# Two blocks of a transformer on one core: the closing norm by halves of the tokens, with GpSimd in the centring, and one ScalarE copy for both groups' turned probabilities

## The reference, cut to what matters

```python
p_s = masked_softmax(s_s, (kpos <= t[:, None])[:, :, None])
o_s = jnp.einsum('bghqn,bgqnd->bghqd', p_s.astype(v_sel.dtype), v_sel)
...
p_w = masked_softmax(s_w, wmask)
o_w = jnp.einsum('bghqk,bgkd->bghqd', p_w.astype(v_w.dtype), v_w)
```

```python
def layer_norm(x, g, b):
    xf = x.astype(jnp.float32)
    mu = jnp.mean(xf, axis=-1, keepdims=True)
    var = jnp.mean(jnp.square(xf - mu), axis=-1, keepdims=True)
    return ((xf - mu) * lax.rsqrt(var + LN_EPS) * g + b).astype(x.dtype)

x = layer_norm(ALPHA * x + sqrelu_mlp(x, mlp_w1[i], mlp_w2[i]), ln2_g[i], ln2_b[i])
```

## Time and profile before

| | us |
|---|---|
| median of 3 runs (1921.96 to 1923.71) | 1922.18 |
| the profiled execution, its own time | 1923.41 |
| its span, first to last instruction | 1921.6 |
| PE busy | 1884.6 (98%) |
| PEld busy | 1516.7 (79%) |
| POOL busy | 1077.0 (56%) |
| DVE busy | 794.2 (41%) |
| ACT busy | 431.5 (22%) |
| mean granted TensorE clock | 0.996 |

### The profile page before, as it was taken

One profiled execution on the slowest core, in us unless ns is written; L12 is line 12 of the kernel. 1 busy time (PEld: TensorE's weight loads), 2 busy tenths in 40 slices (PEclk: granted clock), 3 DMA queues, 4 the chain that ended last, 5 costly groups with the idle time before them and its releaser, 6 DMA issues.

```text
span 1921.6 us, 24551 instructions
## 1 busy us (share of the span) xinstructions
PE 1884.6 (98%) x9032; PEld 1516.7 (79%) x9032; DVE 794.2 (41%) x1305; ACT 431.5 (22%) x850; POOL 1077.0 (56%) x622
## 2 busy tenths in 40 slices
PE   7999999999999999999999999999999999999997
PEld 5878887888888888866778888887776878888885
DVE  6774432352433435688451212126523561212126
ACT  5223422310000121155140101014424140101022
POOL 5756752676657666420556556664752646666552
PEclk9999999999999999999999999999999999999998
DMA  6322321233324225210223322332321223332321
GB/s 231 112 75 92 109 89 33 88 111 100 107 77 132 93 94 199 66 45 1 77 78 98 98 87 87 97 100 76 100 88 45 77 77 99 102 98 95 98 88 44
DMA packets 46880, 176.01 MB, mean 92 GB/s; under 512 B 5200, under 2 KB 5328, under 8 KB 46032
## 3 DMA queue, kind: packets, MB, share of 16 engines
q1 hardware_dynamic: 46512, 169.55, 27.5%
q10 hardware_dynamic: 288, 5.31, 0.7%
HBM read 172.74 MB, written 2.10 MB: 91 GB/s over the span
## 4 chain that ended last, share of the span: by engine, by line
PE 95%; DVE 3%; ACT 1%; issue 1%; DMA 0%; SPq 0%; DVEq 0%
PE acc L499 17%; PE acc L500 17%; PE acc L501 17%; PE acc L526 6%; PE acc L523 6%; PE acc L522 6%; PE acc L578 1%; PE acc L579 1%; PE acc L580 1%; PE acc L1122 1%; PE acc L1124 1%; PE acc L1123 1%; PE acc L598 1%; PE acc L599 1%; PE acc L597 1%; PE misc L831 1%
## 5 line engine op out<-in xcount | busy, mean ns | idle before, releaser
L2491 POOL TENSOR_SCALAR w_hi<-raw 128x1024 fp32r<-128x1024 f32 x309 | 334.8, 1083 | 786.9 <-PE acc L526 292.9
L2493 POOL TENSOR_TENSOR w_lo<-raw,w_hi 128x1024 fp32r<-128x1024 f32 x309 | 746.9, 2417 | 25.8
L499 PE MATMUL acc<-x_hi,w_hi 128*128 128x512 f32 x872 | 343.1, 393 | 0.0
L501 PE MATMUL acc<-x_hi,w_lo 128*128 128x512 f32 x872 | 339.5, 389 | 0.0
L500 PE MATMUL acc<-x_lo,w_hi 128*128 128x512 f32 x872 | 339.4, 389 | 0.0
L1877 DVE TENSOR_TENSOR h<-acc,h 128x512 f32<-128x512 f32 x120 | 82.9, 691 | 365.3 <-PE acc L501 234.4
L499 PE MATMUL acc<-y_hi,w_hi 128*128 128x512 f32 x580 | 227.3, 392 | 0.0
L501 PE MATMUL acc<-y_hi,w_lo 128*128 128x512 f32 x580 | 225.7, 389 | 0.0
L500 PE MATMUL acc<-y_lo,w_hi 128*128 128x512 f32 x580 | 225.7, 389 | 0.0
L499 PEld LDWEIGHTS acc<-x_hi,w_hi 128*128 128x128 f32 x872 | 163.8, 188 | 35.7 <-issue 2.3
L501 PEld LDWEIGHTS acc<-x_hi,w_lo 128*128 128x128 f32 x872 | 163.6, 188 | 34.1
(11 more groups left out here) (430 smaller groups left out, 2738.0 us busy)
## 6 DMA issues: line engine op xcount, KB each, us to landing
raw<-weights_dram SPq DMA_DIRECT2D x309, 512.0 KB, 3.5
w_cmp<-w_cmp_dram ACTq DMA_DIRECT2D x1, 4096.0 KB, 16.0
h<-x_dram SPq DMA_DIRECT2D x2, 1024.0 KB, 6.1
out_dram<-h SPq DMA_DIRECT2D x8, 256.0 KB, 2.0
small<-small_dram SPq DMA_DIRECT2D x1, 1408.0 KB, 15.9
small<-small_dram ACTq DMA_DIRECT2D x1, 1088.0 KB, 5.1
mem_in<-mem_dram SPq DMA_DIRECT2D x1, 1024.0 KB, 12.9
const<-const_dram SPq DMA_DIRECT2D x1, 640.0 KB, 9.1
```

The source lines that it names most:

```text
L499: mm(out, m["w_hi"][:, slot, k], hi[:, k], start=k == 0, stop=False)
L501: last = mm(out, m["w_lo"][:, slot, k], hi[:, k], start=False, stop=k == kc - 1)
L2491: nc.gpsimd.tensor_scalar(hi, m["raw"][:, slot], 1.0, 0.0, ALU.mult, ALU.add).then_inc(sem("weights_high"), 1)
L2493: nc.gpsimd.tensor_tensor(m["w_lo"][:, slot].rearrange("p k n -> p (k n)"), m["raw"][:, slot], bf(hi), ALU.subtract).then_inc(sem("weights ...
```

## The change

**In the batch loop** VectorE's copy is gone. ScalarE copies both groups in one instruction, which waits until both are turned, and one semaphore `n_pt` takes the place of two.

**At the end** `last_tiles`, `last_sums` and two functions called `last_ln` take the place of the second half of the last MLP group and of `residual_ln`, for the last norm alone:

- t12 to t15 are made twice, first for tokens 0 to 255 and then for tokens 256 to 511, with products of 256 columns: 192 in place of 96. A tile of the second half waits until the same tile of the first half has been added to `h` (`last_taken`).
- The sums over the features are made by halves: those of the first half stand behind t12 of the second half.
- ScalarE copies the first mean to `mean` in SBUF. VectorE centres chunks 0 to 3 with it, and GpSimd, behind its last split, chunks 4 to 7 (L2691, 128x512). VectorE adds chunk 4 + j only when GpSimd has centred it (`pool_centred`).
- In the second centring VectorE has chunks 0 to 4 and GpSimd 5 to 7 (`POOL_CENTRES`, L2695, 128x256), for each half.
- `part`, the running squares and the scaled chunks are in SBUF now (`last`, laid over `x_hi` and `x_lo`, which are no longer read then). So these VectorE instructions have two tensors in SBUF as operands: L1977, L1979, L1982, L1983, L1852 (before L1760), L2000, L2003, L2012, L2026 and L2037.
- The result goes out as 16 transfers of 128 KB.

```diff
@@ n_turn, n_values (PE)
-            if b:
-                pe.wait_ge(sem("n_pt%d" % g), b)
+            if b and g == 0:
+                pe.wait_ge(sem("n_pt"), b)
...
-        for g in range(2):
-            pe.wait_ge(sem("n_pt%d" % g), b + 1)
+        pe.wait_ge(sem("n_pt"), b + 1)
@@ batch loop (ACT)
-        act.wait_ge(sem("n_turned"), 2 * b + 1)
+        act.wait_ge(sem("n_turned"), 2 * b + 2)
         if b >= 2:
             act.wait_ge(sem("n_values"), b - 1)
-        f(m["pt_n"][:, b % 2, 0, 0:n], misc[:, 0, 0:n], ACT.Copy).then_inc(sem("n_pt0"), 1)
+        f(m["pt_n"][:, b % 2, :, 0:n], misc[:, 0:2, 0:n], ACT.Copy).then_inc(sem("n_pt"), 1)
@@ batch loop (DVE)
-        dve.wait_ge(sem("n_turned"), 2 * b + 2)
-        if b >= 2:
-            dve.wait_ge(sem("n_values"), b - 1)
-        v.tensor_copy(m["pt_n"][:, b % 2, 1, 0:n], misc[:, 1, 0:n]).then_inc(sem("n_pt1"), 1)
@@ the last tiles (PE)
+    def last_sums(half):
...
+        pe.wait_ge(sem("ln_sum"), 2 * i + 2 + half)
...
+        mm(mean, ones, m["sum_h"][:, cols], start=True, stop=False)
+        pe.wait_ge(sem("last_taken"), HALF * (half + 1))
+        mm(mean, ones, m["h"][:, KC - 1, cols], start=False, stop=True).then_inc(sem("ln_mean"), 1)
+        pe.wait_ge(sem("last_added"), HALF * (half + 1))
+        mm(squares, ones, m["sum_sq"][:, cols], start=True, stop=True).then_inc(sem("last_summed"), 1)
+    def last_tiles(t0, norm):
+        for half in range(2):
+            cols = blk(half, TOK)
+            for j in range(HALF):
+                slot = (t0 + j) % RING
+                if half == 0:
+                    claim(t0 + j)
+                else:
+                    pe.wait_ge(sem("last_taken"), j + 1)
+                for k in range(KC):
+                    mm(acc[:, slot, cols], m["w_hi"][:, slot, k], y_hi[:, k, cols], start=k == 0, stop=False)
+                    mm(acc[:, slot, cols], m["w_hi"][:, slot, k], y_lo[:, k, cols], start=False, stop=False)
+                    last = mm(acc[:, slot, cols], m["w_lo"][:, slot, k], y_hi[:, k, cols], start=False, stop=k == KC - 1)
+                last.then_inc(sem("last_done"), 1)
+                if half == 0 and j == 0:
+                    sum_features(norm, 0)
+                if half == 1 and j == 0:
+                    last_sums(0)
+        last_sums(1)
@@ last_ln (ACT), its first mean and its final steps
+        f(m["mean"], misc[:, 0, :], ACT.Copy, scale=-1.0 / (HALF * P)).then_inc(sem("last_mean"), 1)
...
+        def final(half, k):
+            cols = blk(half, TOK)
+            act.wait_ge(sem("last_scaled"), KC * half + k + 1)
+            f(m["h"][:, k, cols], scaled[:, k, cols], ACT.Identity, bias=pr.col("ln2_b", KC + k))\
+                .then_inc(sem("out_ready"), 1)
@@ last_ln (DVE), the steps ahead of the first take
+        dve.wait_ge(sem("last_mean"), 1)
+        for k in range(HALF):
+            v.tensor_tensor(h[:, k], h[:, k], mean, ALU.add).then_inc(sem("ln_centred"), 1)
+        own.mark(v.scalar_tensor_tensor(part, mean, float(HALF), total, ALU.mult, ALU.add))
+        own.settle()
+        for k in range(1, HALF):
+            add_squares(name, k)
+        def taken(half, j):
+            c, cols, n = HALF + j, blk(half, TOK), HALF * half + j
+            if half == 0:
+                dve.wait_ge(sem("pool_centred"), j + 1)
+            dve.wait_ge(sem("last_done"), n + 1)
+            v.tensor_tensor(h[:, c, cols], acc[:, (t0 + c) % RING, cols], h[:, c, cols], ALU.add)\
+                .then_inc(sem("last_taken"), 1)
...
@@ behind the last split (POOL)
+    pool.wait_ge(sem("last_mean"), 1)
+    for k in range(HALF, KC):
+        nc.gpsimd.tensor_tensor(m["h"][:, k], m["h"][:, k], m["mean"], ALU.add).then_inc(sem("pool_centred"), 1)
+    for half in range(2):
+        pool.wait_ge(sem("last_mean"), half + 2)
+        for k in POOL_CENTRES:
+            nc.gpsimd.tensor_tensor(m["h"][:, k, blk(half, TOK)], m["h"][:, k, blk(half, TOK)],
+                                    m["mean"][:, blk(half, TOK)], ALU.add).then_inc(sem("pool_centred"), 1)
```

More of the change, by code:

```diff
@@ L357, in memory_map @@
     place("row_M", [S], F32, arena - 4 * S)
+    place("last", [KC + 2, S], F32, x)
     place("mn_hi", [KC, MEM], F32R, y)
@@ L410, in norm_banks @@
             return self.misc[:, 0, MEM:2 * MEM], self.misc[:, 0, 0:n], [self.misc[:, b, 0:n] for b in (3, 1, 2)]
+        if name == LAYER_NORMS[-1]:
+            return self.m["last"][:, 0], self.misc[:, 2], None
         fourth = (START[BEFORE_STAGE[name]] + 3) % RING
@@ L1080, in normed_stage @@
         sum_features(norm, 1)
+    def last_sums(half):
+        i, cols = len(LAYER_NORMS) - 1, blk(half, TOK)
+        pe.wait_ge(sem("ln_sum"), 2 * i + 2 + half)
+        mean, squares = misc[:, (1, 3)[half], cols], misc[:, (2, 0)[half], cols]
+        mm(mean, ones, m["sum_h"][:, cols], start=True, stop=False)
[22 more added lines that the diff above has]
+        last_sums(1)
     def mlp_group(name, g, norm, high, next_norm=None):
@@ L1333, in keep, with last_ln, squares, deviation @@
                 .then_inc(sem("norm_kept"), 1)
-        def final(k):
-            f(m["h"][:, k], banks[k % 3], ACT.Identity, bias=pr.col(bias, at + k)).then_inc(sem("out_ready"), 1)
-        if name in KEPT:
-            high_chunks(name, high, keep)
-        else:
-            high_chunks(name, final, None)
+        high_chunks(name, high, keep)
+    def last_ln(name):
+        logs()
+        i, rstd, scaled = LAYER_NORMS.index(name), m["last"][:, 0], m["last"][:, 2:]
+        act.wait_ge(sem("ln_mean"), 2 * i + 1)
+        f(m["mean"], misc[:, 0, :], ACT.Copy, scale=-1.0 / (HALF * P)).then_inc(sem("last_mean"), 1)
+        for k in range(HALF):
+            act.wait_ge(sem("ln_centred"), HALF * i + k + 1)
+            square(name, k, m["h"])
+        def squares(half, j):
+            cols = blk(half, TOK)
+            act.wait_ge(sem("last_taken"), HALF * half + j + 1)
+            if j < 2:
+                act.wait_ge(sem("norm_added"), chunks_before(name) + HALF)
+            else:
+                act.wait_ge(sem("last_added"), HALF * half + j - 1)
+            f(m["sq"][:, j % 2, cols], m["h"][:, HALF + j, cols], ACT.Square).then_inc(sem("last_sq"), 1)
+        def deviation(half):
+            cols = blk(half, TOK)
+            act.wait_ge(sem("ln_mean"), 2 * i + 2 + half)
+            act.wait_ge(sem("last_added"), HALF * half + 3)
+            mean = misc[:, (1, 3)[half], cols]
+            f(m["sq"][:, 0, cols], mean, ACT.Square, scale=1.0 / D).then_inc(sem("ln_mean_sq"), 1)
+            act.wait_ge(sem("pool_centred"), HALF)
+            f(m["mean"][:, cols], mean, ACT.Copy, scale=-1.0 / D).then_inc(sem("last_mean"), 1)
+            act.wait_ge(sem("ln_var"), i + 1 + half)
+            own.link(f(rstd[:, cols], rstd[:, cols], ACT.Ln, bias=LN_EPS, scale=1.0))
+            f(rstd[:, cols], rstd[:, cols], ACT.Exp, scale=-0.5).then_inc(sem("last_rstd"), 1)
+        def final(half, k):
+            cols = blk(half, TOK)
+            act.wait_ge(sem("last_scaled"), KC * half + k + 1)
+            f(m["h"][:, k, cols], scaled[:, k, cols], ACT.Identity, bias=pr.col("ln2_b", KC + k))\
+                .then_inc(sem("out_ready"), 1)
+        for j in range(HALF):
+            squares(0, j)
+        squares(1, 0)
+        deviation(0)
+        squares(1, 1)
+        for k in range(3):
+            final(0, k)
+        squares(1, 2)
+        for k in range(3, 6):
+            final(0, k)
+        squares(1, 3)
+        for k in range(6, KC):
+            final(0, k)
+        deviation(1)
+        for k in range(KC):
+            final(1, k)
@@ L2374, in mlp @@
         up(GROUPS - 1)
-        residual_ln(norm, START[name] + 16 * (GROUPS - 1) + 8, lambda c, first=None: down(GROUPS - 1, c, first))
+        close = last_ln if norm == LAYER_NORMS[-1] else residual_ln
+        close(norm, START[name] + 16 * (GROUPS - 1) + 8, lambda c, first=None: down(GROUPS - 1, c, first))
     mlp("mlp_a", "ln2a")
@@ L2530, in sync_program @@
             .then_inc(sem("weights_in%d" % slot), 16)
-    for k in range(KC):
-        sp.wait_ge(sem("out_ready"), k + 1)
-        sp.dma_start(dram["out"][:, k], m["h"][:, k]).then_inc(sem("stored"), 16)
-    sp.wait_ge(sem("stored"), 16 * KC)
+    for half in range(2):
+        cols = blk(half, TOK)
+        for k in range(KC):
+            sp.wait_ge(sem("out_ready"), KC * half + k + 1)
+            sp.dma_start(dram["out"][:, k, cols], m["h"][:, k, cols]).then_inc(sem("stored"), 16)
+    sp.wait_ge(sem("stored"), 16 * 2 * KC)
 def build(nc, dram):
```

103 lines of the change are left out of this document (93 added, 10 removed).

## The result

| | before | after |
|---|---|---|
| median, us | 1922.18 (1921.96 to 1923.71) | 1926.01 (1925.2 to 1928.49) |
| the profiled execution, its own time | 1923.41 | 1926.01 |
| its span | 1921.6 | 1924.0 |
| from VectorE's first take of the last eight tiles to the end of the span | 1921.6 - 1875.75 = 45.85 | 1924.0 - 1870.76 = 53.24 |

The ratio is 1.0021 with an interval of 1.0015 to 1.0027 (19 runs of each kernel): 3.8 us slower. The whole interval lies above 1, so the loss is real, but it has the 0.2% that the prediction calls no change (1.0020) inside it. The forecast was 2.2 us slower, 1924.4. The last line of the table is the measure to use for the end. It leaves out what happens earlier in the program, and that scatters: where the code ahead of the last tiles was the same, the first take came anywhere between 1870.4 and 1872.2 us.

A forecast was written before the change was run, and what follows sets the result against it. PE was taken as the bound, its chain covering 95% of the span. From 1922.2: -3.6 in the batch loop, +4.5 at the end, +1.3 for the clock, +2.2 in sum, gives 1924.4 us; whole range 1915.5 to 1927.5.

The forecast's parts named there:

- The batch loop: Batch loop: without VectorE's copy 3.6 us are gained (1.4 + 1.1 + 0.4 + 0.7); bounds 0 and 5.4.
- the bound that I name: Three-block batches of the loop: VectorE needs 2.65 us, so PE at 2.71 is the bound, in place of 3.12.
- The rival in which this copy eats the gain: Batch loop: each turn waits for ScalarE's wide copy, gain under 2 us; with none 1928.0, slower. Chance 0.15.
- What stands between the halves: Last tiles: VectorE and GpSimd take turns, the first take ends at 1899.9, and PE stands still for 5.2 us.
- The walk: Last tiles: following the engines' order with turns, GpSimd has 9.9 us of work and VectorE's eight instructions end at 1899.5.
- rows 9: Profile rows before: beside GpSimd, six VectorE instructions with two SBUF operands take 7.65 us where 6 x 0.6 would do.
- The rule that I weighed: GpSimd's centrings at the end: the rule would give 1.4 us each and about 0.7 us more gap; forecast used 1.2.
- The second half and behind it: End: half tiles done at 1913.0 against 1904.05; 9.0 us lost before PE's last product, 4.4 gained behind, 4.5 lost.
- the two terms of the prediction: Behind PE's last product: 3.4 us from take to variance, 7.2 us for centrings, scalings and last activation; against 15.1 before.
- The clock: Behind PE's pause the granted clock falls, half the pace for some 3.5 us; 1.3 us lost, bounds 0 and 2.5.
- The engines do not meet: End: VectorE is not held by GpSimd's centrings, the second half starts without a gap; 1915.8, faster. Chance 0.18.
- The clock holds: End: the granted clock does not fall over PE's gap, the rest as forecast; 1923.1. Chance 0.17.

The follow-up runs named there:

- the run in PSUM: Changed kernel with VectorE's scratch operands at the end in PSUM in place of SBUF, GpSimd's centring kept: median 1915.45 us over 11 runs (ratios 0.9967 and 0.9966).
- the pause filled: Changed kernel with 6 products on PE, whose result nobody reads, added ahead of the second half: 1924.10 us (1.0012).

## Why the prediction was right, and where it was off

**The batch loop**: 3.6 us forecast, 3.85 in the profiles, 3.9 in the run with this part alone. Turns 2.67 us apart for 2.7, the wide copy 1.03 for 1.0. By the bound that I name, PE at 2.71, a batch gains 0.41 and not the 0.45 that I summed; 3.12 - 2.67 gave 0.45 all the same. The rival in which this copy eats the gain is out: it holds up PE for 1.9 us in all.

**What stands between the halves.** The mechanism held in every part: the two engines take turns, the first take is late, PE pauses for 5.3 us (forecast 5.2) with VectorE's take as releaser, and t15 waits 0.8 for its split (0.7). The walk had the right end but not all its steps: it has 13.35 us for the eight instructions, 1.67 each, and the four centrings took 8.03 / 4 = 2.01 and the three sums of squares 4.04 / 3 = 1.35; GpSimd's centrings took 1.70 for about 1.6. After the first take of the stretch, the late take ended at 24.5 us, forecast 24.15. Some of this closeness is luck: the terms that I list for GpSimd, 1.3 + 1.1 + 2.4 + 4 x 1.2, add up to 9.6 us and not to the 9.9 that I went on with, and the 0.3 too much made up for centrings that take 1.27 and not 1.2 by themselves.

That rows 9 could be carried over rests on what kind of instruction meets. The Trainium skill states this in SBUF — State Buffer, section "Who interferes with whom": a VectorE instruction with two SBUF inputs contends with a GpSimd one that reads SBUF, whoever starts first has the shared port for the whole instruction, and one with at most one SBUF input, outside the two-port modes, doesn't contend. The traces agree with both halves of it: 2.01 us with two, 0.62 with one, beside the same kind of GpSimd work.

The rule that I weighed, that an elementwise step with two inputs is about twice as slow on GpSimd as on VectorE (the Trainium skill, GPSIMD Engine Reference, 4.1, Engine selection), is borne out by the run in PSUM, 1.27 us against 0.62. The sum goes by the row: 1.27 is near the 1.2 that I took from half a split. And yet the advice that I drew from it, against this placement, fails there: twice as slow beside VectorE was worth 2.1 us.

**The second half and behind it.** From the next tile to the last sums 8.82 us, forecast 8.64; behind them 10.85 for 10.7 (the two terms of the prediction, 3.4 and 7.2, are 10.6). Both signs as forecast: 11.6 lost ahead of the last sums, 4.2 gained behind.

**The clock is the term that was mis-sized**: 1.3 us forecast (bounds 0 to 2.5), 1.9 measured with the pause filled. I had put half the pace over 3.5 us, from the start of the program, and set part of it off against VectorE's squares. Here half the pace lasted through the whole tile, 5.29 us for 2.88, and 0.5 of the 2.4 lost there was hidden behind VectorE. These 0.6 us, the late take (0.35), the pace of the other tiles (0.2) and the last stretch (0.15) are 1.3 of the 1.6 us by which the end (+7.4) passed its forecast (+5.8); the loop gave 0.3 back.

**The rivals.** "The engines do not meet" was given 1915.8; the kernel in which they don't took 1915.45. That checks the walk without turns, and not that rival's reason: there GpSimd is not kept out, the two just don't meet. "The clock holds" was 1923.1, 1.3 below the forecast; with the pause filled it was 1.9 below the result.

What stays open: a part of 10.6 us of difference between the changed kernel and the one with operands in PSUM. The pause (5.3), the late split (0.8), the half pace (2.4) and the closing stretch (10.85 - 9.47 = 1.4) make 9.9; the rest is some 0.7. Idle time counts from the modelled end of a product, though. From start to start, 0.12 us for a product taken off, the pause is 5.45 and the late split 0.91. With 0.1 for the slower product behind the late split, 1.25 for 1.11 us at the first half's sums, and 0.1 at the product of the first mean, 0.1 us stays open.

**The whole.** Both parts came out with the forecast sign, -3.85 for -3.6 and +7.4 for +5.8. The net of +3.8 stands against a forecast of +2.2 mainly because of the second. Whether this is a change within 0.2%, to which I gave 0.56, the runs do not settle: 1.0021, with 1.0020 inside the interval.

## What to carry to other kernels

Before work is moved to GpSimd, look where the operands of VectorE's instructions beside it lie. The helper was free here only while VectorE had at most one SBUF operand; moving scratch from PSUM to SBUF in the same edit turned a gain of 2.3 to 2.8 us at the end into a loss of 7.5. When a change has two parts, time each alone: a net of +3.8 hid a gain of 3.9. And when a pause of PE has one releaser, ask what that engine's whole queue ahead of it took; moving the releasing step forward only moved the pause.

## What the runs showed that I had not expected

- How long a turn is depends on its partner. Of VectorE's four centrings, the one that stood behind GpSimd's short part of a split took 1.52 us and the one behind the next long part 2.87. Among GpSimd's centrings VectorE's instructions took 1.57 to 1.78, the third sum of squares, behind the last of them, 0.69. With GpSimd at rest, or with one operand in PSUM, four in a row take 0.62 each.
- In the changed kernel PE had stood still for 4 us when the clock fell; at the end of the kernel before it fell 1.5 us behind a few last products that already stood apart from each other. I had gone by the shorter of the two and still priced the fall too low.
- A product with the matrix of ones in plain fp32 is two rows of 0.43 us for 512 columns. A weight product of the same width is one row, 0.227 us from start to start.
